# Feed-forward layers: one pair of output units per round as seven block products, inner channels in two parts

## What is computed

```python
D_MODEL = 1024; SEQ = 512
D_FF = ((-(-8 * D_MODEL // 3)) + 255) // 256 * 256      # 2816

def swiglu_ffn(h, w1, w3, w2):
    return (jax.nn.silu(h @ w1) * (h @ w3)) @ w2
```

## Time and profile before

| | |
|---|---|
| time, median of 3 runs | 2156.87 us (2156.05 to 2160.04) |
| profiled execution, its own time | 2161.26 us |
| its span | 2159.5 us |
| PE busy | 2138.0 us, 99% of the span |
| PEld, DVE, ACT, POOL busy | 1755.8, 949.3, 877.7, 906.1 us |
| mean granted clock of PE | 0.994 |

### The profile page before, as it was taken

One profiled execution on the slowest core, in us unless ns is written; L12 is line 12 of the kernel. 1 busy time (PEld: TensorE's weight loads), 2 busy tenths in 40 slices (PEclk: granted clock), 3 DMA queues, 4 the chain that ended last, 5 costly groups with the idle time before them and its releaser, 6 DMA issues.

```text
span 2159.5 us, 29386 instructions
## 1 busy us (share of the span) xinstructions
PE 2138.0 (99%) x10741; PEld 1755.8 (81%) x10741; DVE 949.3 (44%) x1392; ACT 877.7 (41%) x1325; POOL 906.1 (42%) x463
## 2 busy tenths in 40 slices
PE   8999999999999999999999999999999999999997
PEld 6888888888888888888878888888888888888886
DVE  3206555643364222124974333222788874333211
ACT  3415555743243222234564322223666753333222
POOL 3322333344435444454854444443333334444442
PEclk8999999999999999999999999999999999999999
DMA  8221222166533222333122222233222212222231
GB/s 307 69 68 59 79 78 69 55 220 211 174 139 107 97 97 83 88 99 114 41 98 97 97 97 92 80 93 104 79 79 78 68 61 98 96 97 95 80 97 68
DMA packets 63809, 216.41 MB, mean 100 GB/s; under 512 B 7104, under 2 KB 8256, under 8 KB 62592
## 3 DMA queue, kind: packets, MB, share of 16 engines
q1 hardware_dynamic: 63744, 215.55, 30.2%
HBM read 213.42 MB, written 2.10 MB: 100 GB/s over the span
## 4 chain that ended last, share of the span: by engine, by line
PE 92%; DVE 3%; ACT 2%; issue 1%; DMA 1%; SPq 0%; DVEq 0%; ACTq 0%
PE ps L552 27%; PE ps L554 27%; PE ps L553 27%; PE ps L783 1%; PE ps L784 1%; PE ps L782 1%; PE ps L877 1%; PE ps L1125 1%; PE ps L887 1%; DMA ada_w<-in_w_ada_first 1%; DVE acc L2070 1%; DMA x_res<-in_x 1%; PE ps L630 0%; PE ps L1039 0%; PE ps L1037 0%
## 5 line engine op out<-in xcount | busy, mean ns | idle before, releaser
L399 POOL TENSOR_TENSOR w_lo<-w_raw,w_hi 128x1024 fp32r<-128x1024 f32 (+2 forms) x376 | 843.9, 2253 | 1149.7 <-ACT w_hi L1259 1148.9
L552 PE MATMUL ps<-h_hi,w_lo 128*128 128x512 f32 x1824 | 726.1, 398 | 1.5 <-DVE h_lo L1780 1.2
L554 PE MATMUL ps<-h_hi,w_hi 128*128 128x512 f32 x1824 | 711.4, 390 | 0.0
L553 PE MATMUL ps<-h_lo,w_hi 128*128 128x512 f32 x1824 | 711.3, 390 | 0.0
L1259 ACT ACTIVATE w_hi<-w_raw 128x1024 fp32r<-128x1024 f32 (+2 forms) x376 | 370.7, 995 | 597.3 <-PE ps L554 525.5
L552 PEld LDWEIGHTS ps<-h_hi,w_lo 128*128 128x128 f32 x1824 | 342.9, 188 | 81.4 <-issue 8.1
L554 PEld LDWEIGHTS ps<-h_hi,w_hi 128*128 128x128 f32 x1824 | 343.0, 188 | 72.7
L553 PEld LDWEIGHTS ps<-h_lo,w_hi 128*128 128x128 f32 x1824 | 343.2, 188 | 70.2 <-issue 1.0
L552 PE MATMUL ps<-gu_hi,w_lo 128*128 128x512 f32 x528 | 205.4, 389 | 0.0
L553 PE MATMUL ps<-gu_lo,w_hi 128*128 128x512 f32 x528 | 205.4, 389 | 0.0
L554 PE MATMUL ps<-gu_hi,w_hi 128*128 128x512 f32 x528 | 205.4, 389 | 0.0
(11 more groups left out here) (411 smaller groups left out, 2521.3 us busy)
## 6 DMA issues: line engine op xcount, KB each, us to landing
w_raw<-in_w_ffn_in SPq DMA_DIRECT2D x132, 512.0 KB, 3.4
w_raw<-in_w_hg SPq DMA_DIRECT2D x40, 512.0 KB, 3.4
w_raw<-in_w_ffn_out SPq DMA_DIRECT2D x48, 384.0 KB, 3.1
w_raw<-in_w_conv_gate SPq DMA_DIRECT2D x32, 512.0 KB, 3.5
w_raw<-in_w_merge SPq DMA_DIRECT2D x32, 512.0 KB, 4.6
ada_w<-in_w_ada SPq DMA_DIRECT2D x32, 512.0 KB, 4.5
w_raw<-in_w_ffn_out SPq DMA_DIRECT2D x48, 320.0 KB, 2.9
w_raw<-in_w_cp SPq DMA_DIRECT2D x20, 512.0 KB, 3.6
```

Source lines behind the costliest of these rows:

```text
L399: pool.tensor_tensor(w_lo[s][:, 0:n], raw[s][:, 0:n], w_hi[s][:, 0:n].bitcast(F32), ALU.subtract).then_inc(lo_done[s], 1)
L552: pe.matmul(out, wl, hi, start=first, stop=False)
L553: pe.matmul(out, wh, lo, start=False, stop=False)
L554: return pe.matmul(out, wh, hi, start=False, stop=last)
```

## The change

Rounds before `WINO_FROM` stay as they were. From there on (rounds 3 to 5 and 7 to 10 in layer 0, 2 to 5 and 7 to 10 in layers 1 and 2) units 0 and 1 are computed as before, and units 2 and 3 together as one product of a 2x2 block matrix: the weights (two units by two halves of the input channels) times the activations (two halves of the channels by two halves of 256 tokens). Winograd's form of Strassen's algorithm needs seven block products for it in place of eight, and sums of blocks: T1 to T4 of the activations, made once per layer, and four of the weights, made in every such round. Here is the core of it, engine by engine. The tables and tiles (`wf` are the four half slots of `w_hi` and `w_lo` 2 and 3; `w11` to `w22` the halves of `raw` 2 and 3):

```diff
-FFO = [6, 6, 5, 5]
-FFO_AT = [0, 6, 12, 17]
+HIDDEN = [(0, 6), (6, FC // 2)]
+OUT_TILES = [6, 5]
+WINO_FROM = [[3, 7], [2, 7], [2, 7]]
+C11, C12, C21, C22 = 2, 3, 6, 7
+HT, HK = T // 2, KC // 2
...
+        wf_hi = [w_hi[2 + f // 2][:, f % 2 * (D // 2):(f % 2 + 1) * (D // 2)] for f in range(4)]
+        wf_lo = [w_lo[2 + f // 2][:, f % 2 * (D // 2):(f % 2 + 1) * (D // 2)] for f in range(4)]
+        w11, w12, w21, w22 = (raw[s][:, k * (D // 2):(k + 1) * (D // 2)] for s in (2, 3) for k in range(2))
```

PE:

```diff
+            def term(f, bank, b, add=False):
+
+                for k in range(HK):
+                    w = slice(k * P, (k + 1) * P)
+                    hi, lo = b(k)
+                    out = ps[:, bank, 0:HT]
+                    pe.matmul(out, wf_lo[f][:, w], hi, start=(k == 0 and not add), stop=False, skip_group_check=add)
+                    pe.matmul(out, wf_hi[f][:, w], lo, start=False, stop=False, skip_group_check=add)
+                    mm = pe.matmul(out, wf_hi[f][:, w], hi, start=False, stop=(k == HK - 1), skip_group_check=add)
+                return mm
...
+            def winograd(half, r, q):
+
+                at = side(e, half, r)
+                pe.wait_ge(S["ffn_val0"], r + 11 * e)
+                pe_unit(pe, 0, 0, q, h_hi, h_lo)
+                pe.wait_ge(S["ffn_val1"], r + 11 * e)
+                pe.wait_ge(S["side_lo"], at.lo + 1)
+                term(0, C11, block(0, 0)).then_inc(S["side_mm"], 1)
+                pe.wait_ge(S["side_val"], at.val + 5)
+                term(1, C12, summed(T2)).then_inc(S["side_mm"], 1)
+                pe.wait_ge(S["side_val"], at.val + 6)
+                term(2, C21, summed(T3)).then_inc(S["side_mm"], 1)
+                term(3, C22, summed(T1)).then_inc(S["side_mm"], 1)
+                pe_unit(pe, 1, 1, q, h_hi, h_lo)
+                pe.wait_ge(S["side_val"], at.val + 8)
+                pe.wait_ge(lo_done[2], q + 1)
+                term(0, C11, block(1, 0), add=True).then_inc(S["side_mm"], 1)
+                pe.wait_ge(S["side_val"], at.val + 11)
+                term(1, C12, block(1, 1), add=True).then_inc(unit_done[2], 1)
+                pe.wait_ge(S["side_val"], at.val + 12)
+                pe.wait_ge(lo_done[3], q + 1)
+                term(2, C21, summed(T4), add=True).then_inc(unit_done[3], 1)
```

DVE: the activations' sums (`terms`, a batch in each of the two rounds before the first block round of a layer), the weights' sums (w_x is the third and later the fourth, w21 the first, w_y the second), and the round:

```diff
+            def terms(batch):
...
+                for out, k in ((h_up, 2 * batch), (h_down, HK + 2 * batch)):
+                    dve.tensor_tensor(out[:, :, :], h_hi[:, k:k + 2, :].bitcast(F32), h_lo[:, k:k + 2, :].bitcast(F32), ALU.add)\
+                       .then_inc(S["side_val"], 1)
...
+            def sums_3_1(half, r, q):
+
+                for s in (2, 3):
+                    dve.wait_ge(raw_full[s], 16 * q + 16)
+                dve.tensor_tensor(w_x[:, :], w11, w21, ALU.subtract).then_inc(S["side_val"], 1)
+                dve.tensor_tensor(w21, w21, w22, ALU.add).then_inc(S["side_val"], 1)
...
+            def low_of(half, r, f, v, n):
+                dve.wait_ge(S["side_hi"], side(e, half, r).hi + n)
+                dve.tensor_tensor(wf_lo[f], v, wf_hi[f].bitcast(F32), ALU.subtract).then_inc(S["side_val"], 1)
...
+                join(ps[:, C22, 0:HT], p_five, C21)
+                if e:
+                    scale_up(0, r, q)
+                value(0, r, q)
+                if not final:
+                    sums_3_1(half, r + 1, q + 1)
+                low(0, r, g)
+                if not final:
+                    sum_2(half, r + 1, q + 1)
+                    low_of(half, r + 1, 3, w21, 1)
+                if e:
+                    scale_gate(1, r, q, True)
+                if not final:
+                    low_of(half, r + 1, 1, w_y[:, :], 3)
+                if e:
+                    scale_up(1, r, q, True)
+                value(1, r, q, True)
```

ACT (`weights` writes the high parts for the next round; `between` is the silu of pair 1) and POOL, which makes the low part of w11 and, later in the round, of w12 and w22:

```diff
+            def weights(half, r, q, first, between):
...
+                act.activation(wf_hi[3], w21, ACT.Copy).then_inc(S["side_hi"], 1)
...
+                act.activation(wf_hi[0], w11, ACT.Copy).then_inc(S["side_hi"], 1)
...
+                act.activation(wf_hi[1], w_y[:, :], ACT.Copy).then_inc(S["side_hi"], 1)
+                between()
...
+                act.activation(wf_hi[2], w_x[:, :], ACT.Copy).then_inc(S["side_hi"], 1)
...
+            def low_11(r):
+                pool.wait_ge(S["side_hi"], side(e, half, r).hi + 2)
+                pool.tensor_tensor(wf_lo[0], w11, wf_hi[0].bitcast(F32), ALU.subtract).then_inc(S["side_lo"], 1)
...
+                pool_lo(pool, 0, q + 1, n)
...
+                pool.tensor_tensor(wf_lo[0], w12, wf_hi[0].bitcast(F32), ALU.subtract).then_inc(lo_done[2], 1)
+                pool.wait_ge(hi_done[3], q + 1)
+                pool.tensor_tensor(wf_lo[2], w22, wf_hi[2].bitcast(F32), ALU.subtract).then_inc(lo_done[3], 1)
+                pool_lo(pool, 1, q + 1, n)
+                if not last:
+                    low_11(r + 1)
```

More of the change, by code:

```diff
@@ L1014, in pe_cp @@
+            first()
+            for half, (r0, r1) in enumerate(HIDDEN):
+                for r in range(max(r0, 1), WINO_FROM[e][half]):
+                    hidden(r, h_ready(pe, h_base + KC) if (e, r) == (0, 1) else None)
+                with pe.Fori(WINO_FROM[e][half], r1) as r:
+                    winograd(half, r, r + (q_hidden(e, r0) - r0))
+                output(half)
         def pe_cp(pe):
@@ new lines, in hidden @@
+            def hidden(half, r, batch=None):
+                q, g = q_hidden(e, r), 2 * r - 12 * half
+                for p in range(2):
+                    gate(p, r, q)
+                    for s in (2 * p, 2 * p + 1):
+                        if p == 0 or r + 1 < WINO_FROM[e][half]:
+                            act_hi(act, s, q + 1)
+                    gated(p, r, g + p)
+                    if p == 0 and batch is not None:
+                        terms(batch)
+                if r + 1 == WINO_FROM[e][half]:
+                    weights(half, r + 1, q + 1, True, lambda: None)
@@ L1578, in act_cp @@
+            act_resid(act, i, q_out(e, 1), resid_base, 2, sizes, last, gain, twice)
         def act_cp(act):
@@ new lines, in dve_ffn @@
+            for half, (r0, r1) in enumerate(HIDDEN):
+                first = WINO_FROM[e][half]
+                for r in range(r0, first):
+                    hidden(half, r, None if half or r < first - 2 else r - (first - 2))
+                step = q_hidden(e, r0) - r0
+                with dve.Fori(first, r1 - 1) as r:
+                    winograd(half, r, r + step)
+                winograd(half, r1 - 1, r1 - 1 + step, True)
+                if half:
+                    continue
+                for n in range(KC):
+                    dve.wait_ge(unit_done[n % 2 * 2 + 1], q_out(e, 0) + n // 2 + 1)
+                    if gate is None:
+                        ins = dve.tensor_tensor(x[:, n, :], ps[:, 4 + n % 2, :], x[:, n, :], ALU.add)
+                    else:
+                        ins = dve.scalar_tensor_tensor(out=x[:, n, :], in0=ps[:, 4 + n % 2, :], scalar=gate[:, n:n + 1],
+                                                       in1=x[:, n, :], op0=ALU.mult, op1=ALU.add)
+                    ins.then_inc(S["side_val"], 1)
```

458 lines of the change are left out of this document (331 added, 127 removed).

## The result

The changed kernel takes 2172.4 us in the median of 4 runs (2169.2 to 2173.4), the kernel before 2157.3 us of 4 (2156.1 to 2160.0): a ratio of 1.0066 with a 95% interval of 1.0048 to 1.0083. The change makes the kernel slower by 0.7%.

A forecast was written before the change was run, and what follows sets the result against it. PE, busy 99%, was taken to bound the kernel. Terms -18.4 + 6.0 + 16.2 + 6.1 + 3.4 = +13.3 us, added to the median of 2156.87, gave 2170.2 us, slower by 0.6%; range 2149 to 2184.

The forecast's parts named there:

- waits that exceed the gain: Main case: PE's waits in the block rounds cost more than fewer columns save; 57%, own range 2161 to 2180 us.
- fewer columns, 23 rounds: Units 2 and 3: 84 matmuls of 256 columns (10.08 us) replace 48 of 512 (10.88 us); -18.4 us over 23 rounds.
- later block rounds, layers 1 and 2: Block rounds behind another block round: PE waits 0.5 us for the second pair's value, 12 times; +6.0 us.
- slot 2 and first block rounds, layers 1 and 2: Batches of sums delay DVE: PE waits 1.2 us for slot 2 and 6.9 us before block products, twice; +16.2 us.
- other first rounds: First block rounds without a batch directly ahead, and layer 0's first half: 2 x 1.8 + 1.1 + 1.4 = +6.1 us.
- clock: PE at half clock behind the two 6.9 us gaps, about 1.7 us lost each; +3.4 us, bounds 0 and 5 us each.
- The weight loads: Rival: loads don't overlap, so block products take 16.0 us a round; +117 us, 2274; 3% together with the late reload.
- the 0.5 without a row: Later block rounds, layers 1 and 2: PE restarts near 10.3 us after unit 1's end, 0.5 us late.
- the rival with 5 us for each of four gaps: Rival: long half clock behind gaps of 6.9 and 1.8 us in layers 1 and 2; +20 us, 2187; 7%.
- Engines keep up: Rival: POOL holds DVE only now and then, later rounds don't wait, waits stay under 14 us; 2146; 20%.
- signs: In the changed profile: DVE's w_x at 2 to 3 us instead of 0.69, two side_lo waits of 6 to 8 us.
- late reload: Rival: weights' sums wait for raw 2 and 3, landing after over 6.1 us; 2200; 3% together with loads pacing.

The follow-up runs named there:

- value first: Changed kernel, with VectorE's low part of w_y moved behind the second pair's scaling and value in every block round that another follows: 2166.0 us, ratio 1.0037 to before.
- best version: Changed kernel with block rounds from round 3 in layers 1 and 2, second pair's value before w_y's low part, weights' sums and rounding earlier: 2143.2 us, 0.9941 to before.
- sums early, from 2: Changed kernel, with only the last direct round reordered: weights' sums (VectorE) and rounding of two weight blocks (ScalarE) before the second pair's value: 2158.7 us, 1.0008 to before.
- gap filled: Changed kernel plus 26 unread 512-column matmuls in each of layers 1 and 2, while PE waits before its first block product: 2169.3 us, 1.0056 to before.
- small sums: Changed kernel, with activation sums of layers 1 and 2 over 8 columns instead of 256, same instruction count, output different: 2151.8 us, 0.9975 to before.

## Why the prediction was right

It said 2170.2 us for its likeliest case, waits that exceed the gain. Term by term, predicted and then what the trace of the changed kernel has beyond PE's pace:

| term | predicted | measured | read from |
|---|---|---|---|
| fewer columns, 23 rounds | -18.4 | -17.5 | 21.00 us from one block round to the next without waits ("value first"), 21.76 for a direct one |
| later block rounds, layers 1 and 2 | +6.0 | +4.7 | 21.39 us instead of 21.00, 12 times |
| slot 2 and first block rounds, layers 1 and 2 | +16.2 | +14.7 | 2 x (1.17 + 6.16) |
| other first rounds | +6.1 | +4.6 | 2 x 1.42 + 1.01 + 0.70 |
| clock | +3.4 | +4.2 | 2 x 2.1 |
| not foreseen: `acc`, DVE's sum of squares for the norm in front of layer 0 | 0 | +0.9 | wait of 1.2 us, was 0.35 |
| sum | +13.3 | +11.6 | |

The spans differ by 8.0 us, or 13.0 with the 5.0 that only the execution of before lost at its start; 1.4 us more than the rows explain. The medians differ by 15.1. So no term was off by more than 1.5 us, and the direction and the size are those of the terms; but the sum came as near to the median as it did partly because waits priced 4.3 us too high stand in for losses of clock that the profiled execution doesn't have: it ran at 0.994, the other three at 0.991 to 0.993. That part of the agreement is luck.

*The gain.* The best version bears it out: 21 block rounds at 0.76 are 16.0 us, less 1.4 us of gaps and about 0.5 for `acc` 14.1; the last column of the table fell by 13.6 to 13.9. The weight loads did not pace the short matmuls, which start 0.120 us apart here as in the earlier trace rows. The Trainium skill (TensorE: Matmul & The Clock Gate, Back-to-back issue gap) leads to an estimate of 98 ns for them; the runs disagree with it as the trace of before did.

*Later rounds.* In the round shown under "value first", unit 1 ended at 1219.53 and PE wanted the value 9.78 us later; the value came at 9.94, where the prediction had 9.95, and PE was back at 10.07, where it had 10.3. Those last 0.35 us from the value to PE's restart stand in the 0.5 without a row; the trace has 0.13. The order of events was as told (w_x held, low part of w_y held, then scaling and value), with one thing more in it: the reload landed some 4.6 us after POOL's piece in that round, not 3.4, and w_x waited for it, but under the hold that it would have met anyway. The chain that was priced is the chain in the trace. POOL's piece, behind which the reload of the `w_x` of 1222.47 (shown above) is issued, and the one that holds `w_x` until 1223.41 (it ends at 1223.97):

```profile
1216.44 1.29 POOL L490 TENSOR_TENSOR w_lo<-w_raw,w_hi 128x512 fp32r<-128x512 f32 x1
1220.93 2.48 POOL L465 TENSOR_TENSOR w_lo<-w_raw,w_hi 128x1024 fp32r<-128x1024 f32 x1 [3.20 <-ACT w_hi L1413]
```

"Value first" shows that the order of DVE's queue is enough to take the wait away, with the reload as late as before.

*The first block rounds.* The mechanism is shown from two sides: without the batches' time the gap is 1.4 us, and with the batches a round later 2.5. The late root (`rstd` of round 0), by which the working begins, only matters through the batch that follows it.

*The clock.* The sign and the place were right. The loss per gap was 2.1 us where 1.7 was taken from the earlier trace rows, and both gaps of 6.2 us had it; the rival with 5 us for each of four gaps is out, since nothing fell behind the gaps of 1.4 us.

*Engines keep up.* DVE took 0.69 us for `w_x` in 11 of the 23 rounds: in all of layer 0 and in the first block rounds, where POOL stood idle or began behind it (1180.80). In the 12 later rounds of layers 1 and 2, the very ones that were priced with a wait, it took 1.4 to 1.8 us, and 2.9 in two. So the holds came where they were forecast, but mostly shorter than the 2 to 3 us that the signs named, since the late reload let `w_x` start later under POOL's piece. No run takes POOL's piece away; the hold is read from these durations. The Trainium skill (SBUF — State Buffer, Who interferes with whom) says that a VectorE instruction with two SBUF inputs contends with a GpSimd instruction that reads SBUF; the trace agrees, by these durations.

*Slips in the recorded sums.* 1192.9 - 1186.1 is 6.8 and not 6.9. The first half of layer 0 was to be taken like a term of 1.1 and was given 1.4 (the trace has 1.01). Block products break even at 10.88 / 84 = 0.1295 us each and not at 0.128. The 2200 of the late reload doesn't follow from 21 rounds of 2 us, which would make 2212. The first two move the forecast by 0.2 and 0.3 us, the others not at all.

## What to carry to other kernels

When a change trades work on a full engine for work on others, their average load says little: here DVE, busy for 54%, let PE wait and lose clock for 29 us against a gain of 17.5, nearly all of it where its queue stood in the wrong order: the best version, with the same arithmetic in two rounds fewer, keeps 13.6 of 16.0 us. Write down for each instruction when its input is ready and when somebody needs its output; here the inputs of the weights' sums lay ready several microseconds before the sums were issued, and moving those sums and the value, with the batches a round later, turned a loss of 0.7% into a gain of 0.6%. Place one-time work (the batches) where the engine has had no other reason to be late, even if that gives up a round of the new form.

## What was not expected of the hardware

In the changed kernel the granted clock fell to 0.50 while PE was still waiting, 1.9 us before it took up work again, and stayed there for 4.9 us of work. In "sums early, from 2" it fell 0.5 and 0.2 us after PE had taken up work. Only the part under work costs. The Trainium skill (TensorE: Matmul & The Clock Gate, Terms) puts the penalty at half the throttled time, an estimated 3.4 us for 6.8; the trace disagrees, with 2.1 us behind each gap, since 1.9 us of the stretch fell on the wait and the 23 matmuls in the rest took 0.213 us each, which is less than twice 0.120. In the feed-forward layers it fell behind every gap of 6.2 and 3.4 us, behind one of four of 2.5 us, and behind none of 1.4 or 0.7 us. Late in the attention it fell behind a gap of 1.66 us in three of ten profiled executions (before, changed, value first). It fell once each behind a gap of 1.6 us earlier in that stage ("gap filled", at 1607 us) and behind the wait for `acc` in front of layer 0's feed-forward ("small sums", 1.1 us), a wait that seven other executions have at 0.8 to 1.3 us without it. So the length of a gap alone doesn't tell whether the clock falls. PE kept at work with matmuls that nobody reads kept it at 1.00.

Runs of one kernel differ mostly by this clock. Of the kernel before, single runs lie between 2154.9 and 2164.2 us, while time x granted clock has a standard deviation of 0.7 us, of which the three digits of the clock alone make about 0.6. The other kernels have 0.7 to 1.7. For differences under 0.3% the mean of that product is the sharper number, with the reserve that it forgives half clock under a wait.
